# A decoder step on one core: pair order of the scores and transposes, a shorter forget bias, and an earlier paged softmax

## What is computed

```
logits = q @ k^T / 8 + f[query] - f[key]      # f = cumsum of log sigmoid forget values, branch A
p      = softmax(logits, causal);  o = p @ v
```

## Time and profile before

| | |
|---|---|
| median of 3 runs | 1567.37 us (1563.78 to 1569.9) |
| profiled execution | 1567.51 us, span 1565.7 us |
| TensorE busy | 1419.9 us, 91% of the span |
| mean granted clock | 0.949 |
| forget bias | about 193.5 to 213.3 us |
| attention A on the prompt | 213.3 to 303.5 us, with two projections at its end |
| projections with paged values | 303.5 to 443.8 us |
| attention C on the prompt | 466.6 to 554.6 us |

### The profile page before, as it was taken

The page is one execution under the profiler, slowest core; times in us unless marked ns, Lnnn a source line. Parts: engine busy times, 40 slices in busy tenths (PEclk is TensorE's granted clock), DMA queues, the critical chain, the costliest instruction groups (busy, mean ns, idle before and its releaser), DMA issues.

```text
span 1565.7 us, 20000 instructions
## 1 busy us (share of the span) xinstructions
PE 1419.9 (91%) x7544; PEld 1068.0 (68%) x7544; DVE 743.7 (47%) x1302; ACT 432.2 (28%) x721; POOL 309.0 (20%) x233
## 2 busy tenths in 40 slices
PE   7999978799998899999999999999938799999980
PEld 3466465444454599999999999878736466666650
DVE  1266445422124442243443444455666466777746
ACT  1111134201015411111111111212124455665536
POOL 1138920045174000000000000000231521221220
PEclk9969999999999999999999999999958899999995
DMA  7346630255331022232222332422376999888645
GB/s 219 104 134 222 207 127 1 71 172 186 132 99 42 35 77 72 77 104 77 73 93 77 106 142 77 145 78 81 120 300 256 312 302 305 289 300 272 202 164 221
DMA packets 75196, 237.70 MB, mean 152 GB/s; under 512 B 17029, under 2 KB 27476, under 8 KB 61422
## 3 DMA queue, kind: packets, MB, share of 16 engines
q1 hardware_dynamic: 48630, 160.73, 28.4%
q0 software_dynamic: 17792, 59.20, 12.8%
q10 hardware_dynamic: 8704, 16.84, 3.1%
HBM read 213.49 MB, written 65.74 MB: 178 GB/s over the span
## 4 chain that ended last, share of the span: by engine, by line
PE 75%; DMA 8%; DVE 6%; POOL 4%; ACT 3%; issue 3%; SPq 0%; POOLq 0%; DVEq 0%; ACTq 0%
PE ps L460 15%; PE ps L462 14%; PE ps L461 14%; PE ps L1224 11%; DMA tmp_yd<-b,b 7%; PE ps L1205 5%; PE ps L593 4%; POOL b L1967 3%; PE ps L1321 2%; PE ps L1358 2%; PE ps L1409 1%; ACT b L1590 1%; PE ps L522 1%; PE ps L1221 1%; PE ps L1239 1%
## 5 line engine op out<-in xcount | busy, mean ns | idle before, releaser
L460 PE MATMUL ps<-b,b 128*128 128x344 f32 (+1 forms) x1360 | 470.3, 346 | 9.3 <-DVE b L987 3.8
L461 PE MATMUL ps<-b,b 128*128 128x344 f32 (+1 forms) x1360 | 465.8, 342 | 0.0
L462 PE MATMUL ps<-b,b 128*128 128x344 f32 (+1 forms) x1360 | 465.8, 342 | 0.0
L460 PEld LDWEIGHTS ps<-b,b 128*128 128x128 f32 x1360 | 255.2, 188 | 30.8 <-issue 10.7
L462 PEld LDWEIGHTS ps<-b,b 128*128 128x128 f32 x1360 | 255.1, 188 | 19.4 <-issue 0.9
L461 PEld LDWEIGHTS ps<-b,b 128*128 128x128 f32 x1360 | 255.0, 188 | 17.0 <-issue 0.6
L1224 PE MATMUL ps<-b,b 128*128 128x512 f32 (+1 forms) x640 | 258.1, 561 | 0.0
L1224 PEld LDWEIGHTS ps<-b,b 128*128 128x128 f32 x640 | 122.3, 194 | 121.7 <-issue 117.1
L1056 POOL DMA_INDIRECT tmp_xs<-b,b x36 | 44.9, 1247 | 634.4 <-issue 574.9
L1205 PE MATMUL ps<-b,b 128*128 128x128 f32 (+1 forms) x782 | 122.8, 286 | 51.0 <-DMA b<-tmp_xs 18.6
L987 DVE TENSOR_TENSOR b<-b,b 128x2048 fp32r<-128x2048 f32 x64 | 146.3, 2289 | 45.3 <-ACT b L678 42.7
(11 more groups left out here) (265 smaller groups left out, 1261.9 us busy)
## 6 DMA issues: line engine op xcount, KB each, us to landing
b<-in_w SPq DMA_DIRECT2D x96, 1024.0 KB
b<-in_w_merge SPq DMA_DIRECT2D x32, 640.5 KB, 4.5
tmp_xs<-b ACTq DMA_DIRECT2D x32, 514.0 KB, 4.0
b<-tmp_xs SPq DMA_DIRECT2D x32, 514.0 KB
b<-in_w_in SPq DMA_DIRECT2D x8, 1024.0 KB, 8.6
b<-in_xT SPq DMA_DIRECT2D x4, 1024.0 KB, 12.4
b<-in_w_out SPq DMA_DIRECT2D x4, 1024.0 KB, 7.7
b<-in_x SPq DMA_DIRECT2D x8, 512.0 KB, 4.0
```

The source lines that it names most:

```text
L460: mm(out, hi, mhi, start=start, stop=False)
L461: mm(out, hi, mlo, start=False, stop=False)
L462: return mm(out, lo, mhi, start=False, stop=stop)
```

## The change

Four edits, in one step.

1. *Pair order.* TensorE does scores(u+1), values(u/2-1), scores(u+2) and then the four transpose groups of u and u+1. ScalarE takes the exponentials of u+1, then the copies of u and u+1, then the exponentials of u+2; the upper blocks (bank 5) of odd units are copied by ScalarE (`high_blocks`), those of even units still by VectorE.
2. *Forget bias.* One product of `ones_neg` with all of `lpre` (32 columns, bank 3) gives the sums over the tiles before; VectorE copies them once, and adds them with a broadcast operand as it moves each group to `fb`. The second product per tile is gone.
3. *Paged softmax.* Its steps are spread over attention A: `side_a` and `softmax_step` on VectorE, `side_a` on TensorE (products into spare columns of bank 7), the exponential on ScalarE behind the pair of unit 8.
4. *Slots.* `values_a(s)` moves from slot s+3 to slot s, and the three softmax steps of branch C from slots 13 to 15 to slots 11 to 13.

GpSimd's and SP's lists are unchanged.

```diff
-        SLOTS_A = {i: ["top", "spread", "total"][i:i + 1] if i < 3 else [i - 3] for i in range(18)}
+        SLOTS_A = {i: [i] if i < 16 else [] for i in range(18)}
         for i, step in enumerate(("top_c", "spread_c", "total_c")):
-            SLOTS_A[13 + i].append(step)
-        SLOTS_A[17].append(15)
+            SLOTS_A[11 + i].append(step)
...
                     for q in range(4):
-                        t = half * 4 + q
-                        o_ = ps[:, 6 + n % 2, q * P:(q + 1) * P]
-                        mm(o_, lf[:, t, h:h + 1].to_broadcast([P, P]), tri_neg[:], start=True, stop=(t == 0))
-                        if t:
-                            m = mm(o_, lpre[:, t, h:h + 1].to_broadcast([P, P]), ones_neg[:], start=False, stop=True)
+                        m = mm(ps[:, 6 + n % 2, q * P:(q + 1) * P], lf[:, half * 4 + q, h:h + 1].to_broadcast([P, P]), tri_neg[:],
+                               start=True, stop=True)
                     m.then_inc(S("fb_mm"), 1)
                     n += 1
+                    if n == 2:
+                        mm(ps[:, 3, 0:32], ones_neg[:], lpre[:].rearrange("p t h -> p (t h)"), start=True, stop=True).then_inc(S("fb_mm"), 1)
...
                 scores(0)
-                for u in range(16):
-                    if u < 15:
-                        scores(u + 1)
-                    if u % 2 == 0 and u:
+                for u in range(0, 16, 2):
+                    scores(u + 1)
+                    if u:
                         values(u // 2 - 1)
-                    transposes(u, 0)
-                    transposes(u, 1)
+                    if u < 14:
+                        scores(u + 2)
+                    for v in (u, u + 1):
+                        transposes(v, 0)
+                        transposes(v, 1)
...
+            def side_a(i):
+                if i == 2:
+                    pe.wait_ge(S("dmx"), 1)
+                    tr(ps[:, 7, W:W + P], mx[:]).then_inc(S("dmx_tr"), 1)
+                elif i == 3:
+                    pe.wait_ge(S("dmc"), 1)
+                    mm(ps[:, 7, W:W + 32], mcol[0:32, 0:1].to_broadcast([32, P]), ident[0:32, 0:32],
+                       start=True, stop=True).then_inc(S("dmb"), 1)
+                elif i == 5:
+                    pe.wait_ge(S("dsum"), 1)
+                    mm(ps[:, 7, W:W + 32], ones[:], dsum[:], start=True, stop=True).then_inc(S("dtot"), 1)
...
-                for u in range(16):
+                for u in range(0, 16, 2):
+                    weights(u + 1, 0)
+                    weights(u + 1, 1)
+                    blocks(u, 0)
+                    blocks(u, 1)
                     for hh in range(2):
-                        blocks(u, hh)
-                        if u < 15:
-                            weights(u + 1, hh)
+                        blocks(u + 1, hh)
+                        high_blocks(u + 1, hh)
+                    if br == 0 and u == 8:
+                        act.wait_ge(S("dsh"), 1)
+                        act.activation(sA[:], sA[:], ACT.Exp).then_inc(S("dex"), 1)
+                    if u < 14:
+                        weights(u + 2, 0)
+                        weights(u + 2, 1)
...
             for n in range(8):
-                dve.wait_ge(S("fb_mm"), n + 1)
-                dve.tensor_copy(fb[:, n // 2, (n % 2) * 512:(n % 2) * 512 + 512], ps[:, 6 + n % 2, :]).then_inc(S("fb"), 1)
+                if n >= 2:
+                    dve.wait_ge(S("fb_mm"), n + 2)
+                first = dsum[:].rearrange("p (t h) -> p h t", h=H)[:, n // 2, 4 * (n % 2):4 * (n % 2) + 4]
+                dve.tensor_tensor(fb[:, n // 2, (n % 2) * 512:(n % 2) * 512 + 512].rearrange("p (t r) -> p t r", r=P),
+                                  ps[:, 6 + n % 2, :].rearrange("p (t r) -> p t r", r=P),
+                                  first.rearrange("p (t o) -> p t o", o=1).to_broadcast([P, 4, P]), ALU.add).then_inc(S("fb"), 1)
...
-            decode_softmax(0, sA, lambda: qk_evict("qkc", 1, 1), lambda: None)
+            qk_evict("qkc", 1, 1)
             qk_evict("qkc", 2, 2)
             key_sums_c(0)
             key_sums_c(1)
```

More of the change, by code:

```diff
@@ L1291, in _ @@
             n = 0
+            pe.wait_ge(S("ob"), 5)
             for h in range(H):
@@ L1377, in bias_a @@
                 pe.wait_ge(S("qkT_qka"), 8)
+                pe.wait_ge(S("ltot"), 1)
+                mm(ps[:, 5, 0:32], trisA[:], ltot[:], start=True, stop=True).then_inc(S("lsuf"), 1)
             def tail_a():
@@ L1382, in tail_a @@
                 project("qkc", 0)
-            attention(0, bias_a, lambda k, h: va[:, k, h * 64:h * 64 + 64], lambda i: None, tail_a)
+            def side_a(i):
[9 more added lines that the diff above has]
+                    mm(ps[:, 7, W:W + 32], ones[:], dsum[:], start=True, stop=True).then_inc(S("dtot"), 1)
+            attention(0, bias_a, lambda k, h: va[:, k, h * 64:h * 64 + 64], side_a, tail_a)
             def top(br):
@@ L1430, in heads_out @@
                 m.then_inc(S("heads"), 1)
-            steps = {"top": lambda: top(0), "spread": lambda: spread(0), "total": lambda: total(0),
-                     "top_c": lambda: top(1), "spread_c": lambda: spread(1), "total_c": lambda: total(1)}
+            steps = {"top_c": lambda: top(1), "spread_c": lambda: spread(1), "total_c": lambda: total(1)}
             def decode_slot(i):
@@ L1843, in attention @@
                         norm(u // 2 - 1)
-                    blocks(u, 0)
-                    blocks(u, 1)
+                    if u % 2 == 0:
+                        blocks(u, 0)
+                        blocks(u, 1)
                     side(u)
@@ L1848, in attention, with softmax_step @@
                 return lambda: norm(7)
-            def side_a(n):
-                if n == 1:
-                    key_sums(15)
+            mA = mrow[:].rearrange("p (b o h) -> p b o h", b=NB, o=1).to_broadcast([P, NB, 17, H])
+            rA = drec[:].rearrange("p (b o h) -> p b o h", b=NB, o=1).to_broadcast([P, NB, 17, H])
+            s16 = sA[:, :, 0:16, :]
+            def softmax_step(i):
+                if i == 2:
+                    dve.wait_ge(S("dmx_tr"), 1)
+                    dve.tensor_reduce(mcol[0:32, :], ps[0:32, 7, W:W + P], AX.X, ALU.max).then_inc(S("dmc"), 1)
+                elif i == 3:
+                    dve.wait_ge(S("dmb"), 1)
+                    link(dve.tensor_copy(mrow[:], ps[:, 7, W:W + 32]))
+                    dve.tensor_tensor(sA[:], sA[:], mA, ALU.subtract).then_inc(S("dsh"), 1)
+                elif i == 5:
+                    dve.wait_ge(S("dtot"), 1)
+                    link(dve.reciprocal(drec[:], ps[:, 7, W:W + 32]))
+                    dve.tensor_tensor(sA[:], sA[:], rA, ALU.mult).then_inc(S("dp"), 1)
@@ new lines, in side_a @@
+            def side_a(u):
+                if u == 0:
+                    dve.wait_ge(S("lgb"), 16)
+                    dve.wait_ge(S("lsuf"), 1)
+                    link(dve.tensor_tensor(ltot[:], ps[:, 5, 0:32], lgb[:], ALU.add))
+                    link(dve.tensor_tensor(lfs[:, 0], lfs[:, 0],
+                                           ltot[:].rearrange("p (b o h) -> p b o h", b=NB, o=1).to_broadcast([P, NB, 16, H]), ALU.add))
+                elif u == 1:
+                    key_sums(15)
+                elif u == 2:
+                    dve.wait_ge(S("ks"), 16)
+                    link(dve.scalar_tensor_tensor(s16, s16, SCALE, lfs[:, 0], ALU.mult, ALU.add))
+                elif u == 3:
+                    dve.wait_ge(S("selfd0"), N("selfd0", 16))
+                    link(dve.tensor_scalar(sA[:, :, 16, :], sA[:, :, 16, :], SCALE, None, ALU.mult))
+                    dve.tensor_reduce(mx[:, 0:32].rearrange("p (b h) -> p b h", b=NB), sA[:].rearrange("p b r h -> p b h r"),
+                                      AX.X, ALU.max).then_inc(S("dmx"), 1)
+                elif u == 10:
+                    dve.wait_ge(S("dex"), 1)
+                    dve.tensor_reduce(dsum[:].rearrange("p (b h) -> p b h", b=NB), sA[:].rearrange("p b r h -> p b h r"),
+                                      AX.X, ALU.add).then_inc(S("dsum"), 1)
```

38 lines of the change are left out of this document (14 added, 24 removed).

## The result

The changed kernel takes 1662.6 us (median of 4 runs, 1660.3 to 1664.69), the kernel before, run on the same chip, 1566.51 (4 runs, 1563.78 to 1569.9): ratio 1.0625, 95% interval 1.0594 to 1.0655. It is slower, as forecast, and 5.6 us above the forecast of 1657, inside its range. The profiled execution took 1664.69 us, its span 1662.9, which is 97.2 more than the 1565.7 of before.

A forecast was written before the change was run, and what follows sets the result against it. The prediction took TensorE, busy 91% of the span, as the bound. Its terms, 87.2 + 9 - 8.6 - 4.5 + 3.5 + 2.5 = +89.1, on 1567.5 gave 1656.6, so 1657 us, range 1640 to 1678.

The forecast's parts named there:

- Waits: Projections after attention A: TensorE waits for paged-value gathers, 17.2 us first, then five of 14 us; 87.2 us.
- Restarts: Projections after attention A: low TensorE clock after each of six gaps, 1.5 us each; +9 us (6 to 18).
- Softmax gap: Between attention A and the projections: the nearly idle stretch and the low clock behind it go; -8.6 us.
- Softmax steps in A: Attention A: paged softmax moved in, three extra small TensorE products charged 0.3 us, VectorE's steps mostly hidden.
- Bias: Forget-bias stretch before attention A: 28 products become one, 8.2 us instead of 12.7; -4.5 us (-5.5 to -2).
- Pair order in A: Attention A: more exposed bank 4 handovers, less waiting for VectorE's copy, later start; +3.5 us (0 to +6).
- The relief from VectorE: Attention A: ScalarE copying odd units' upper blocks frees bank 5 earlier, removing waits for VectorE's copy; about -2 us.
- Pair order in C: Attention C: same reordering as in attention A, with shorter scores; +2.5 us (-1 to +5).
- One wait only: Projections with paged values: GpSimd catches up after the first wait; 1579 us, chance 5%.
- loads in time: Projections with paged values: gathers arrive in time, so only the removed gap counts; -7.1 us, 1560 us, chance 4%.
- Long round trips: Projections with paged values: each of the five later waits is 18 us, not 14; +20, 1677 us, chance 5%.
- The clock falls in each burst: Attentions A and C: clock restart behind seven transpose bursts in each, 1.5 us apiece; +21, 1678 us, chance 4%.

The follow-up runs named there:

- keys late: Changed kernel with GpSimd loading and multiplying the keys of s-2 instead of s behind gather s, value steps still in slot s; 1592.72 us, ratio 1.0199 to the kernel before.

## Why the prediction was right

Point by point, by the terms of its sum. The measured ones are taken from the traced executions of before and of the changed kernel, 97.2 us apart: 87.4 + 12.3 - 8.1 in the projections, 6.9 in A, 2.4 in C, -3.3 ahead of A, and 2.1 and -2.5 in pooling and the rest, which the sum had at nothing.

- *Waits, 87.2.* Measured 87.4, in the slots named, none in slot 4. The legs of the round of s = 3 came out as in the sum: 2.2 us from the transposes' end to the first key load (1.9 and 0.3 in the sum), 3.7 to the multiply (3.9), 2.0 to the gather (1.8), 6.05 from there to the value step (5.9). Putting the slots back (89 us less), moving the keys (five waits gone) and moving the first keys (the first wait gone from s = 2) show the place, the loop and the start each by itself.
- *Restarts, +9.* Mis-sized by 3: value steps behind a wait took 1.93 or 2.74 us instead of 1.07 or 1.48 and the projections behind them 7.4 to 8.4 instead of 7.13, as the same steps without a gap took in this trace; 12.3 in all for six, 1.5 to 2.8 each, 2.05 on average and not 1.5. The length of the gap does not order them: in the run with slots s+1 a gap of 5.75 us cost 2.4.
- *Softmax gap, -8.6.* Right in place: the stretch grew by 91.6, so 87.4 + 12.3 leave -8.1 for it. But it only pays with cover. In the run with slots s+3 and the old pair order the stretch is 4.6 shorter than before, because a wait of 2.85 us and the slower projection behind it (8.83 us in the row of slots s+3) turn up at the short slot.
- *Softmax steps in A, 0.3 of its 3.5.* Mis-sized. In three kernels with the old pair order A took 92.9 instead of 90.2 us at a full clock. Of these 2.7, 1.85 are TensorE's own, busy for 80.75 instead of 78.90 us, and 0.8 are waits for VectorE. The products are small, but where they stand alone in PE's timeline they take 0.33 to 0.41 us each (245.99 and 272.38 us in the changed kernel).
- *Bias, -4.5.* A starts 3.3 us earlier (3.3 to 5.0 in the eight kernels with the edit; those without it differ by 1.9 among themselves). Pooling gives back 2.1 (6.4 with the bias alone). That pooling would answer was not forecast. It doesn't always give back all: with slots s+3 and the old pair order A starts 6.0 us earlier with the bias edit than without it, and pooling is 1.2 longer.
- *Pair order in A, +3.5.* Measured +6.9. At a full clock it would have been +3.7, since A took 93.9 us at 1.00 in the run with keys late, which has the same lists there; so the term, softmax steps included, looks right. Its parts are not, and that is luck. The seven more waits for ScalarE are there (the lists behind these points), at 3.6 us for 4.2. The relief from VectorE is 1.1 for 2, the 1.2 at the start is absent (0.49 us at the first handover, 0.45 before), and TensorE works 1.2 us longer on the softmax's products, for 0.3. The other 3.2 of the 6.9 are the clock, which the sum had at nothing: TensorE's busy time is 83.30 us here and 80.10 there.
- *Pair order in C, +2.5.* Measured +2.4. TensorE's idle time grew from 12.2 to 13.9 us: 22 waits for ScalarE, 13.2 us, instead of 16 with 8.9, and 2.3 less for VectorE. The other 0.7 is busy time (75.47 instead of 74.78) at a clock of 0.92 instead of 0.94.

TensorE's waits in A (us in all, how often, the longest), before and then in the changed kernel:

```profile
PE ps L1205 <- ACT b L1590: 9.7, 17, 0.8
PE ps L1205 <- DVE b L1811: 1.2, 2, 0.8
PE ps L1349 <- DVE b L1817: 0.4, 1, 0.4
...
PE ps L1204 <- ACT b L1599: 13.3, 24, 0.8
PE ps L1318 <- DVE b L1829: 0.5, 1, 0.5
```

**The rivals.** *One wait only* and *loads in time* fell. *Long round trips* fell: all five lie between 13.65 and 14.10. *The clock falls in each burst*, held at 4% and +21, came true in part. In the changed kernel two of the seven new bursts in A were followed by the low level, at 1.6 us each where 1.5 was the price. Seven kernels have the new ScalarE order, the changed one among them, and in six of the seven the profiled execution had a clock in A below 1.00; the five with the old order, the kernel before among them, all had 1.00. By TensorE's busy time the price was 2 to 6 us in A, and in C, where the old order has low stretches too (0.94), 1 to 4. The rule that transposes do not count as TensorE being busy (the Trainium skill, TensorE: Matmul & The Clock Gate, Part 4: PE-mode transpose) fits the fall behind the burst at 254 us and not the last and longest burst, where the clock of the changed kernel stayed at 1.00 as in the earlier trace rows. I had let one row with one burst stand for all; that is the step that failed, for some 4 of the 97 us. That the median came within 6 us of the forecast is owed to the waits; that the small terms came so near is in part luck.

What stays open: why the clock in A differs between kernels with the same pair order (93.9 us at 1.00, 100.2 at 0.93; the run with keys late has the burst of the fifth pair with the same waits, 0.66, 0.66 and 0.55 us, and stayed at 1.00 behind it), and what in pooling ties its end to the store of `out_pool_p`. Neither was tried by itself.

## What to carry to other kernels

A slot that a consumer stands behind its load is cover, even where the trace shows no wait: before it is taken away, follow the loader's whole list round once, with every wait in it, and compare the round with what one slot lasts. Here a round was 14 us plus a slot because the gather stood behind a key load that waited for the consumer's own engine; moving the consumer by three places was worth about 90 us and moving the keys by two about 67, while the tuning of the softmax and bias that it was meant to serve was worth less than this measurement can show. Where a stage is fed by another engine's list from a fixed point, arriving earlier uses up cover: here 4.6 us of some 8 were kept with three slots and none with two.

## What was new of the hardware

- The granted clock fell inside an attention stage in which TensorE's waits were short (in the run with the pair order alone 24 for ScalarE, 13.3 us in all, 0.8 the longest): 0.67 on average over 10 us. Waits of 0.45 to 0.66 us between groups of one to six transposes were what preceded the falls, there and in the changed kernel, and the same order of instructions gave 93.9 us at 1.00 in one kernel and 100.2 at 0.93 in another.
- A gap of 14 to 18 us cost 1.5 to 2.8 us more than its length behind it, 2.05 on average over six, and one of 5.75 us cost 2.4.
- A gather of 1 MB issued behind a 128x768 multiply landed 5.5 us after its issue, and a row of 1 KB issued 1.0 us behind it 0.4 us later than the gather. Rounds with a gather, three key loads and a multiply took 8.8 to 9.4 us in the changed kernel and in those with slots s+2 and with keys late, whether or not TensorE waited.
